# Compressed keys and values laid beside their next token by transfers on the chip, sliding keys written twice by GpSimd

## The reference, cut to what matters

```python
def compress(kv, pos_emb, w1, w2):
    n_cmp = (S - CMP_BLOCK) // CMP_STRIDE + 1
    idx = jnp.arange(n_cmp)[:, None] * CMP_STRIDE + jnp.arange(CMP_BLOCK)[None, :]
    blocks = kv[:, idx] + pos_emb[None, None, :, None, :]
    blocks = blocks.transpose(0, 1, 3, 2, 4).reshape(B, n_cmp, G, CMP_BLOCK * Dh)
    return jax.nn.gelu(blocks @ w1) @ w2
```

## Time and profile before

| | us |
|---|---|
| median of 3 runs (1785.93 to 1790.8) | 1785.94 |
| the profiled execution | 1786.98 |
| its span, first to last instruction | 1785.2 |
| TensorE busy | 1699.8 |
| VectorE busy | 932.8 |
| ScalarE busy | 717.3 |
| GpSimd busy | 381.9 |

### The profile page before, as it was taken

The page is one execution under the profiler, slowest core; times in us unless marked ns, Lnnn a source line. Parts: engine busy times, 40 slices in busy tenths (PEclk is TensorE's granted clock), DMA queues, the critical chain, the costliest instruction groups (busy, mean ns, idle before and its releaser), DMA issues.

```text
span 1785.2 us, 24819 instructions
## 1 busy us (share of the span) xinstructions
PE 1699.8 (95%) x9410; PEld 1327.8 (74%) x9410; DVE 932.8 (52%) x1675; ACT 717.3 (40%) x1607; POOL 381.9 (21%) x515
## 2 busy tenths in 40 slices
PE   7999998999879998999999999999999989998989
PEld 6887667877755555888888888888886767886657
DVE  3785664345346766344443244234736664457672
ACT  4324563222336665224431133233335553434550
POOL 5441332012125564011000000000103330022330
PEclk9999998999959999999999999999999999998979
DMA  7222002423012222322333322233330003230011
GB/s 185 95 86 79 25 24 83 142 71 118 24 38 61 59 62 62 129 102 83 96 103 106 95 95 95 95 109 105 96 96 22 27 23 142 95 95 23 26 48 47
DMA packets 107204, 141.37 MB, mean 79 GB/s; under 512 B 30348, under 2 KB 55204, under 8 KB 106848
## 3 DMA queue, kind: packets, MB, share of 16 engines
q1 hardware_dynamic: 106032, 139.10, 24.3%
q0 software_dynamic: 992, 0.86, 0.5%
q10 hardware_dynamic: 80, 0.02, 0.0%
HBM read 125.24 MB, written 4.24 MB: 73 GB/s over the span
## 4 chain that ended last, share of the span: by engine, by line
PE 75%; ACT 10%; DVE 9%; issue 4%; POOL 1%; DMA 0%; ACTq 0%; SPq 0%; POOLq 0%; DVEq 0%
PE ps L1975 55%; PE ps L1967 2%; PE ps L2439 2%; PE ps L2216 2%; DVE nm L1466 2%; PE ps L2237 2%; ACT pbd L932 2%; DVE spl L1138 1%; PE ps L2252 1%; PE ps L2414 1%; ACT pbf L932 1%; ACT pb L876 1%; PE ps L2390 1%; ACT pts L940 1%; ACT qkt L953 1%
## 5 line engine op out<-in xcount | busy, mean ns | idle before, releaser
L1975 PE MATMUL ps<-spl,ht 128*128 128x512 f32 x2496 | 576.5, 392 | 3.0 <-DVE spl L1161 3.0
L1975 PEld LDWEIGHTS ps<-spl,ht 128*128 128x128 f32 x2496 | 471.4, 189 | 102.4 <-DVE spl L1161 3.3
L1161 DVE TENSOR_TENSOR spl<-raw,spl 128x1024 fp32r<-128x1024 f32 x168 | 221.5, 1360 | 401.0 <-ACT spl L711 401.0
L711 ACT ACTIVATE spl<-raw 128x1024 fp32r<-128x1024 f32 x168 | 168.5, 1052 | 489.1 <-PE ps L1975 462.6
L1975 PE MATMUL ps<-ht,spl 128*128 128x512 f32 x960 | 220.2, 391 | 2.0 <-DVE spl L1161 2.0
L1975 PEld LDWEIGHTS ps<-ht,spl 128*128 128x128 f32 x960 | 181.1, 189 | 40.5 <-issue 2.9
L1975 PE MATMUL ps<-spl,uu 128*128 128x512 f32 x768 | 174.7, 389 | 0.0
L1975 PEld LDWEIGHTS ps<-spl,uu 128*128 128x128 f32 x768 | 144.1, 188 | 29.8
L2439 PE MATMUL ps<-ht,spl 128*128 128x512 f32 x576 | 155.0, 408 | 1.6 <-DVE mx L1521 1.6
L1848 POOL TENSOR_TENSOR sq<-qkv 128x2048 f32<-128x2048 f32 (+1 forms) x15 | 51.5, 3435 | 343.8 <-ACT qkv L748 329.2
L2439 PEld LDWEIGHTS ps<-ht,spl 128*128 128x128 f32 x576 | 102.7, 190 | 21.9 <-DVE mx L1521 2.8
(11 more groups left out here) (314 smaller groups left out, 2250.5 us busy)
## 6 DMA issues: line engine op xcount, KB each, us to landing
raw<-w_in SPq DMA_DIRECT2D x30, 1024.0 KB, 5.1
raw<-w_mlp_up SPq DMA_DIRECT2D x16, 1024.0 KB, 5.2
raw<-w_mlp_down SPq DMA_DIRECT2D x16, 1024.0 KB, 5.0
raw<-w_in_a SPq DMA_DIRECT2D x16, 1024.0 KB, 5.3
raw<-w_in_b SPq DMA_DIRECT2D x8, 1024.0 KB, 5.5
raw<-w_proj_diff SPq DMA_DIRECT2D x4, 1024.0 KB, 6.4
stq<-qkv SPq DMA_DIRECT2D x16, 256.0 KB, 2.7
stq<-qkv SPq DMA_DIRECT2D x32, 128.0 KB, 2.5
```

The costliest lines, as they stand in the source:

```text
L711: act.activation(SPL[:, n % 2, HI, 2 * k:2 * k + 2], RAW[:, n % 2, 2 * k:2 * k + 2], ACT.Copy).then_inc(hi_done, 4)
L1161: dve.tensor_tensor(SPL[:, n % 2, LO, 2 * k:2 * k + 2], RAW[:, n % 2, 2 * k:2 * k + 2], SPL[:, n % 2, HI, 2 * k:2 * k + 2].bitcast(F32), A ...
L1975: last = pe.matmul(PS[:, b0 + b], left[:, x], right[:, y], start=(kt == 0 and i == 0), stop=(kt == UK * g["units"] - 1 and i == 2))
```

## The change

The eviction of kc now writes each group of 64 columns with a gap of 64 behind it, into columns 1536 to 2559 of `qkv`. SP then fills the gaps with the same group's numbers of the next token: for each of 4 token tiles one transfer of 127 partitions (from partition p+1 to p, 8 runs of 64 numbers each), and three transfers of one partition (from the next tile's first token to the last partition). They stand in SP's queue after the load of unit 8 and before that of unit 9, behind a wait for kc's eviction. A crossing waits for all seven (`c_pair`) and then needs 4 x 4 transposes of 128 columns. The shift by one column is gone from VectorE's reads. For swa, GpSimd copies each key head twice side by side into columns 2560 to 3071 after skv's norm, and keys are turned by four transposes of 128 columns.

```diff
--- before.py
+++ after.py
@@ -390,7 +390,8 @@
 
             return BESIDE[k], n + (0 if a.is_diff else IN_DIFF[k]) + (IN_FOX[k] if a.is_swa else 0)
 
-        ck_zero = sem("ck_zero")
+        c_pair = sem("c_pair")
+        ck_zero, k_twice = sem("ck_zero"), sem("k_twice")
         x_parked, x_back = sem("x_parked"), sem("x_back")
         c_tr, c_xk, c_hid, c_gelu, c_out, c_link, c_root, c_kb, c_vb, w1_full = [sem(x) for x in (
             "c_tr", "c_xk", "c_hid", "c_gelu", "c_out", "c_link", "c_root", "c_kb", "c_vb", "w1_full")]
@@ -494,6 +495,10 @@
         def row_bank(name):
 
             return 4 * (1 - RUNS["merge"][0]["group"] % 2) + 3 if name == "merge" else 4 * (SIDE[name]["group"] % 2) + 3
+
+        def token_pairs(t):
+
+            return QKV[:, t, 1536:2560].rearrange("p (g r d) -> p g r d", r=2, d=HD)
 
         def reach(eng, s, value):
 
@@ -599,7 +604,14 @@
             sp.wait_ge(y_hi, KT)
             sp.wait_ge(y_lo, KT)
             sp.dma_start(W1[:], I["cmp_k_w1"][0].rearrange("(k p) n -> p k n", p=P)).then_inc(w1_full, 16)
-            weights(RUNS["nsa_in"], skip=6)
+            weights(RUNS["nsa_in"], skip=6, only=3)
+            sp.wait_ge(freed["act"], RUNS["nsa_in"][2]["freed"])
+            for t in range(NT):
+                here, ahead = token_pairs(t), token_pairs(t + 1) if t + 1 < NT else None
+                sp.dma_start(here[0:P - 1, :, 1], here[1:P, :, 0]).then_inc(c_pair, 16)
+                if t + 1 < NT:
+                    sp.dma_start(here[P - 1:P, :, 1], ahead[0:1, :, 0]).then_inc(c_pair, 16)
+            weights(RUNS["nsa_in"], skip=9)
             sp.wait_ge(c_hid, 1)
             sp.dma_start(W1[:], I["cmp_v_w1"][0].rearrange("(k p) n -> p k n", p=P)).then_inc(w1_full, 16)
             weights(RUNS["merge"], only=2)
@@ -745,8 +757,10 @@
                     k = g["late"]
                     act.wait_ge(*row_count(k))
                     for t in range(NT):
-                        last = act.activation(QKV[:, t, then[1]:then[1] + W], PS[:, b0 + t], ACT.Copy,
-                                              scale=RST[:, k, t:t + 1])
+                        dst, src = QKV[:, t, then[1]:then[1] + W], PS[:, b0 + t]
+                        if g["name"] == "kc":
+                            dst, src = token_pairs(t)[:, :, 0], src.rearrange("p (g d) -> p g d", d=HD)
+                        last = act.activation(dst, src, ACT.Copy, scale=RST[:, k, t:t + 1])
                     last.then_inc(freed["act"], 1)
 
             def narrow_in(g):
@@ -1668,7 +1682,7 @@
                     dve.wait_ge(c_hid, 1)
                 b = c_bank(6 if i else 4)
                 for k in range(16):
-                    src = PS[:, b:b + 4, 2 * k + 1:2 * k + 2 + CMP_STRIDE * (N_CMP - 1):CMP_STRIDE]
+                    src = PS[:, b:b + 4, 2 * k:2 * k + 1 + CMP_STRIDE * (N_CMP - 1):CMP_STRIDE]
                     dve.tensor_scalar(XK[:, k], src, POS[:, i, k:k + 1], None, ALU.add).then_inc(c_xk, 1)
 
             def key_norm():
@@ -1929,6 +1943,15 @@
                     square(KT - 1)
                     root(KT - 1)
 
+            def keys_twice():
+
+                pool.wait_ge(n_done, RUNS["swa_in"][0]["normed"] + 1)
+                keys = QKV[:, :, 1024:1280].rearrange("p t (h d) -> p t h d", d=HD)
+                both = QKV[:, :, 2560:3072].rearrange("p t (h r d) -> p t h r d", r=2, d=HD)
+                for r in range(2):
+                    last = pool.tensor_copy(both[:, :, :, r], keys)
+                last.then_inc(k_twice, 1)
+
             def clear_narrow(last):
 
                 pool.wait_ge(unit_used, last["unit"] + last["units"])
@@ -1953,7 +1976,9 @@
             clear_narrow(RUNS["mlp"][-1])
             run(RUNS["fox_in"])
             attend_beside(FOX)
-            run(RUNS["swa_in"])
+            run(RUNS["swa_in"][:1])
+            keys_twice()
+            run(RUNS["swa_in"][1:])
             attend_beside(SWA)
 
 
@@ -2071,18 +2096,13 @@
             def tokens_across(i):
 
 
-                kc = RUNS["nsa_in"][2]
-                pe.wait_ge(freed["act"], kc["freed"])
+                pe.wait_ge(c_pair, 16 * (2 * NT - 1))
                 if i:
                     pe.wait_ge(freed["act"], RUNS["nsa_in"][4]["freed"])
                 for g in range(GROUPS):
-                    b = c_bank(6 if i else 4) + g
-                    src = QKV[:, :, 1024 + 256 * i + HD * g:1024 + 256 * i + HD * g + HD]
+                    b, c = c_bank(6 if i else 4) + g, 1536 + 512 * i + P * g
                     for t in range(NT):
-                        n = P - (t == NT - 1)
-                        pe.transpose(PS[0:HD, b, P * t + 1:P * t + 1 + n], src[0:n, t], IDF[0:n, 0:n])
-                        last = pe.matmul(PS[HD:P, b, P * t:P * t + P], src[:, t], IDF[:], start=True, stop=True,
-                                         skip_group_check=True)
+                        last = pe.transpose(PS[:, b, P * t:P * t + P], QKV[:, t, c:c + P], IDF[:])
                 last.then_inc(c_tr, 1)
 
             def first_layer(i):
@@ -2420,14 +2440,8 @@
                     for t in range(NT):
                         bank, col = (first_bank(a, m, i), P * t) if m < 2 else (turn_bank(a, X_BANK), P * t) if a.is_diff \
                             else (turn_bank(a, PT_BANK + t // 2), 256 + P * (t % 2))
-                        if i == 0 or not a.is_swa:
-                            c = 1024 * i + P * m
-                            last = pe.transpose(PS[:, bank, col:col + P], QKV[:, t, c:c + P], IDF[:])
-                            continue
-                        k = QKV[:, t, 1024 + HD * a.keys_of(m):1024 + HD * a.keys_of(m) + HD]
-                        pe.transpose(PS[0:HD, bank, col:col + P], k, IDF[:])
-                        last = pe.matmul(PS[HD:P, bank, col:col + P], k, IDF[:], start=True, stop=True,
-                                         skip_group_check=True)
+                        c = 2560 + P * a.keys_of(m) if i and a.is_swa else 1024 * i + P * m
+                        last = pe.transpose(PS[:, bank, col:col + P], QKV[:, t, c:c + P], IDF[:])
                     last.then_inc(s["tk" if i else "tq"], 1)
 
                 def side(k, first, end):
@@ -2452,6 +2466,8 @@
                 last_in = RUNS[a.name + "_in"]
                 pe.wait_ge(freed["act"], last_in[-2]["freed"])
                 pe.wait_ge(n_done, last_in[{"diff": 3, "fox": 4, "swa": 1}[a.name]]["normed"] + 1)
+                if a.is_swa:
+                    pe.wait_ge(k_twice, 1)
                 for m, i in a.first_turns()[:3]:
                     turn(m, i)
                 pe.wait_ge(*row_kept(a.name))
```

## The result

The changed kernel takes **1836.72 us**, the median of four runs (1836.33 to 1838.52). Beside it the kernel before took 1788.13 (four runs, 1785.93 to 1790.8). The ratio is 1.0271, interval 1.0253 to 1.0289: slower by 48.6 us. The profiled execution took 1836.98 us, 50.0 us more than the one of before; its span of 1835.1 is 49.9 us longer.

The account below looks back on a forecast made before the run. The prediction took TensorE, busy 95% of the span, as the bound. Terms +70.5 +3.0 -7.7 -2.1 -3.8 gave +59.9 us; on the profiled 1786.98, less 1.0 for the median, 1846 us, range 1835 to 1891.

Parts of the forecast that it names:

- The wait, +70.5: TensorE at the first crossing waits 70.5 us for the four 127-row transfers, all on one engine at 18.3 ns a packet.
- The clock, +3.0: Behind that wait at the first crossing TensorE's clock is low, costing 3.0 us, bounds 1.7 and 3.7.
- First crossing, -7.7: Compressed stage, before unit 7: 16 transposes of 128 columns take 2.0 us instead of 9.67; all 7.7 us count.
- Second crossing, -2.1: Compressed stage, before unit 11: 2.1 us count, 5.6 become a wait for VectorE before kw; bounds 0 and 7.7.
- Sliding keys, -3.8: Sliding attention: three key turns in the loop save 1.25 us each, 3.8 together, the first nothing; bounds 0 and 5.7.
- Copies on GpSimd, 0: After skv's norm: two copies, costing as much as a 3.60 us product, fit a 10 us idle stretch; no change.
- The eviction of kc, 0: Four activations, 2.40 us, storing runs of 64 instead of 512: no change, up to 0.6 us more.
- Rival 1: First crossing: all 16 engines carry the 127 rows, TensorE waits 1 us; sum -12.6, 1773 us; chance 0.12.
- Rival 2: First crossing: one engine per transfer, but different ones side by side; wait 18.6 us, sum +8.0, 1794 us; chance 0.03.
- Rival 3: First crossing: wide transfers, large issues cost SP twice 0.62 us, landing some 5 us late; 1781 us, no difference; chance 0.03.

## Why the prediction was right, and which term was off

The direction, the cause and the place held: 1846 us with a range of 1835 to 1891 were predicted, 1836.72 was measured. The sum was 59.9 us and came out at 49.9 in the spans of the profiled executions: +55.1 (wait) +2.7 (clock) -7.8 (first crossing) -0.1 (second crossing and what follows) -3.4 (sliding keys) +3.4 (outside the change). So one term was 15.4 too large and one 2.0 too small, and the rest is within 0.5 each.

That the time lies inside the range is partly luck. It is 1.7 us above the low end, and that end was built from a packet of 17.7 ns and full gains elsewhere, none of which came; the packet's real price lies below every value in the prediction. Without the 3.4 us from outside the change the time would have been some 1833, by these traces, and outside the range.

- **The wait, +70.5: measured 55.1.** The mis-sized term. That all four transfers run on one engine was right: 18 GB/s throughout, 50 us of wait gone when 112 rows go in place of 127, and no gain from a second queue. Wrong was the price of a packet. I took 18.3 ns from a transfer that runs on 16 engines at once. On one engine alone it is 256 bytes at 18 GB/s, 14.2 ns, or 14.4 ns from the 14.8 us between large transfers (1024 packets). 4064 packets at 3.9 ns less are 15.8 us. From the first issue to the landing it took 61.0 us (359.12 to 420.15), where 76.1 were summed. The transfers started 1.9 us later than I had them (359.12 for 357.25) and TensorE arrived 2.2 us later (365.03 for 362.8), which nearly cancel; the wait fell short by 15.4. The row was of the same size of packet but not of the same number of engines, and the low end of my range (17.7) came from the same row.
- **The clock, +3.0.** Behind the wait the crossing lost 1.7 (3.33 against 1.66 at full clock) and units 7 and 8 another 1.0: 2.7, inside 1.7 to 3.7.
- **First crossing, -7.7.** With the clock's part taken out, 7.8 (9.44 to 1.66).
- **Second crossing, -2.1: measured -0.1.** The wait before kw was foreseen with 5.6 and came with 5.9. What was missed is that a wait of such length costs clock as well, which I had charged for the long wait only: kw's 48 matmuls took 12.71 us, and 14.09 where 112 rows were sent. It is the other wrong step, and it took the whole of this term: 7.8 shorter, 5.9 of wait, 1.8 behind it.
- **Sliding keys, -3.8.** Pairs gave 1.35 each, 1.25 predicted; from the first scores to the end the two traces differ by 3.4. The first turn was worth nothing, and the wait went from 6.95 to 8.91 (8.8 predicted).
- **Copies on GpSimd, 0.** 4.1 us, hidden, with 8 us to spare.
- **The eviction of kc, 0.** Four activations took 2.40 us before, and with gaps of 64 too:

```profile
356.70 2.40 ACT L763 ACTIVATE qkv<-ps,rst 128x512 f32<-128x512 f32 x4
```

- **Not in the sum:** the profiled execution lost 2.0 us ahead of the first crossing, and another 1.4 between the compression's second layer and swa's first scores, on code that is the same. They hid part of the first error. They differ from execution to execution: over all the traces TensorE reaches this crossing between 363.0 and 367.0, and what makes it differ was not looked into.

Rival 1, 16 engines for 127 rows, is refuted by the rate. Its saving needed 112 rows, and its 1 us of wait was 5.3 there (eleven issues) and 2.7 with two queues; its 1773 was passed only by the version that issues the keys first, with the adds early. Rival 2 fell with the two queues. Rival 3, wide transfers with issues twice as long, would need a wide rate, and the rate was 18 GB/s. With 112 rows it was nearest to what came: wide transfers, a wait of 5.3 set by eleven issues, a low clock behind it, and 4.8 us under before. What stays open is why a packet costs 14 ns on one or four engines and 18 to 20 on sixteen: a limit that the engines share would do it, but no run here tells it from others.

## What to carry to other kernels

Look at the number of rows of a transfer before its bytes: 127 rows ran at 18 GB/s, and the same rows cut into 112 and 15 at over 200. Take the price of a packet from a row with the same number of engines at work, and look for two costs of a narrow transfer: the time of its data, and the queue that cannot issue behind it. Once it is wide, the number of issues is the next limit; split it by what is wanted first and not by what lies together. And charge the clock with a short wait on TensorE too: here one of 5.9 us cost 1.5 to 3 us on top, and wait and clock together ate the whole 7.8 us that the crossing had saved. Last, compare traces from place to place: two executions reached the first crossing 3.5 us apart with the same code ahead of it (363.01 and 366.53).

## What the runs showed of the hardware that I had not expected

- A packet of 256 bytes cost 14.2 ns where one engine ran (18 GB/s), 14.0 where four did (73 GB/s), and 18 to 20 ns where sixteen did (200 to 227 GB/s over 16).
- The number of engines was the largest divisor of the rows up to 16 in every run where the share tells: 127 rows at 0.08, 124 at two to three tenths, 120 at eight to nine tenths.
- An issue behind a narrow transfer blocks: 13.8 us behind 1016 packets on one engine, 3.9 us behind 248 on each of four, 26 to 28 us where two queues share the one engine. Where the transfers are wide it took 0.7 to 1.0 us with 112 rows, and up to 1.9 us at the longest.
- TensorE's clock stood at 0.50 for at least the first microseconds behind an idle 5.9 us, and the next 48 matmuls took 12.5 to 14.1 us instead of 11.1. The idle 55 us cost 2.7, no more than the dearest of the short ones: the clock was full again in the stretch from 427 on, 7 us behind the wait. With 112 rows it was still at 0.57 from 447 to 450, as far behind the wait of 5.9:

```profile
443.40:447.00 3.60, 3.60 (x9) 2.83 (x10) 3.60 (x7) 0.00 (x0) 0.48 (x1) 0.50 0.00 0
447.00:450.00 3.00, 3.00 (x9) 2.33 (x8) 2.65 (x7) 0.22 (x1) 0.00 (x0) 0.57 0.91 294
```
